# Piecewise first weight splits, woven indexer steps and merged short query tiles in a hybrid decoder step

## The chip, the cores and the metric

The kernel runs on one core of a Trainium2 chip. The metric is the device time of one execution, in microseconds (us). The core has five engines that run at the same time and meet at semaphores: TensorE (PE: matrix products and transposes; its weight loads are listed as PEld), VectorE (DVE), ScalarE (ACT), GpSimd (POOL) and SyncE (SP, which here only issues DMAs). DMA queues move data between HBM, the large memory, and SBUF, the working memory of 128 partitions; matrix products land in PSUM.

## The reference

One inference step of a two-layer decoder trunk. A prompt of 512 tokens and eight sample sequences of 8 new tokens each (576 tokens in all) go through the same weights; each sample also has 2048 past tokens in paged caches.

```python
D_MODEL, SEQ, DEPTH, DEC_BATCH, DEC_SEQ, PAST_LEN, HEAD_DIM, N_HEADS, H_IDX, D_FF = 1024, 512, 2, 8, 8, 2048, 64, 16, 8, 2816
# layer 0: one input projection -> mixer A (indexer-selected attention, 8 heads) beside mixer B (dilated windows, 8 heads)
# layer 1: one input projection -> mixer C (compressed, selected-block and window branches, 16 heads, gated)
# after each mixer: output projection, layer norm, ConvFFN, layer norm

def dsa_attend(q, qi, wi, q_pos, k, v, ki, tab):          # mixer A; its scores are the indexer
    s = jnp.einsum('bqhe,ble->bqhl', qib, ki) * (D_IDX ** -0.5)
    score = jnp.einsum('bqhl,bqh->bql', jax.nn.relu(s), wib) * (H_IDX ** -0.5)
    score = jnp.where(kpos <= pb, score, -jnp.inf)
    _, idx = lax.top_k(score, top)                        # then softmax attention over the picked keys

def masked_softmax(logits, mask):                         # all mixers; logits carry a bias by distance
    m = jnp.max(logits); p = jnp.exp(logits - m) * mask
    return p / jnp.sum(p)

def ab_project(x, w_in): ... split_cols(x @ w_in, AB_SPLITS)       # c_project likewise
# ConvFFN: up-projection to 2*2816, causal conv of width 3, gelu(gate) * value, down-projection
```

## The kernel before

**Phases.** The kernel is a chain of phases, one after another, with a barrier of all engines at the end of each: `proj_ab` (input projection of layer 0, with the set-up of the whole kernel in front), `tok_ab` (turns some results token-major), `idx` (the indexer), `sb` and `sa` (sample attention of B and A), `pab` (prompt attention of A and B), `out_ab`, `ffn0`, `proj_c`, `tok_c` and a compression step, `pc` (prompt attention of C), `sc` (sample attention of C), `out_c`, `ffn1`. Time saved inside one phase moves all later ones forward.

**Products in three parts.** A float32 product is made from three reduced ones (`split_product`, line 230): high weight by high input, high by low, low by high. The high part of a weight is a cast by ACT, the low part is what the cast left over, a subtraction by DVE (`low_part`, line 227, both of its inputs in SBUF). In `project_phase` ACT casts a group of 128x2048 weights in `split_high` (line 335), DVE subtracts in `split_low`, and `column_block` runs the 48 matmuls (8 k-tiles, 3 products, 2 halves) of 128 output columns, two such blocks to a group. `ffn_phase` has the same pair (line 2189) and `up_block`. PE waits for the whole group's low part before its first matmul. In `proj_ab` POOL meanwhile adds three rows of position tables in the set-up (line 222, 16x2952 each, also from two SBUF operands).

**Indexer (`indexer_phase`).** The past keys of eight samples are gathered page by page by POOL (line 493, eight gathers into four slots); the first four are issued in `tok_ab`. Sixteen half-samples are turned (`turn`, PE), copied (DVE), multiplied with the queries (`dot`, PE) and passed through ReLU (ACT). After every four halves `head_sums` adds the heads into a PSUM bank, DVE copies it to `part` (`copy_part`, line 1047, two buffers), and SP stores it to HBM and loads it back in another order (line 928, eight DMAs each time) into the score rows; there are four such parts in turn, and SP waits for each store to land before its loads. Between them SP issues the first key and value loads of `sb`. After the halves come 24 prompt steps (`prompt_dots`, `p_relu`, and a multiply-add on DVE, line 1071), and then SP stores the prompt scores (line 932). The phase ends when all of it is done.

**Prompt attention (`prompt_attention_phase`, for `pab` and `pc`).** Work units are (pair of heads, query tile i of 128 tokens, part); tile i sees (i+1)x128 keys. `pab` has 8 pairs with one part, `pc` 8 pairs with two. In round u PE runs `scores(u)`, `turn(u-2)` and `values(u-3)`; DVE runs `shift(u)` (line 742, adds the bias, takes the row maximum) and `weigh(u-1)` (a reciprocal at line 754, then scaling at line 759 or 762); ACT copies the turned weights (`copy_turned`, line 714) and runs the exponentials (line 725). `logit` and `shifted` are two deep, `tps` one. The order on each engine is the order of these loops:

```python
for u in range(U + 3):
    if u < U:
        scores(u)
    if 2 <= u < U + 2:
        turn(u - 2)
    if u >= 3:
        values(u - 3)
```

Of the kernel before, what the change touches and what calls it, by code (L numbers as in the profile page):

```python
# [21 lines left out]
P = 128  # L22
# [220 lines left out]

def project_phase(nc, name, w_in, cols, hT, keep, late_stores=(), late_loads=None, setup_of=None, ring=None):
# [8 lines left out]
    with phase(nc, name) as p:  # L253
# [12 lines left out]
        zero_set = p.sem("zero_set")  # L266
        setup = None if setup_of is None else Setup(nc, p, *setup_of)
# [32 lines left out]
        def column_block(pe, n, s, lo, slot):  # L300

            pe.wait_ge(copied0, n + 1)
            pe.wait_ge(copied1, n + 1)
            out = (acc[slot][0][:, 0:TH], acc[slot][1][:, 0:TH])
            for k in range(KC):
                last = split_product(pe, out, wh[:, s, k, lo:lo + P], wl[:, s, k, lo:lo + P], halves(keep.xh, k), halves(keep.xl, k),
                                     k == 0, k == KC - 1)
            last.then_inc(done, 1)

        @block.tensor  # L310
        def _(pe):
# [5 lines left out]
            with pe.Fori(0, loops) as i:  # L317
# [10 lines left out]
        def split_high(act, g, i, s, first=False):  # L328
# [6 lines left out]
            act.copy(wh[:, s, :, :], w[:, s, :, :]).then_inc(high, 1)  # L335

        def split_low(dve, g, s):
# [32 lines left out]
        def _(dve):  # L370
# [9 lines left out]
            for s in range(2):  # L380
                split_low(dve, s, s)
# [18 lines left out]
def token_major_phase(nc, name, hT, pieces, tok, keep, ahead=None):  # L400

    chunks = [(r0 + o, min(P, n - o), c0 + o) for r0, n, c0 in pieces for o in range(0, n, P)]
    with phase(nc, name) as p:
# [14 lines left out]
        if ahead is not None and ahead.other_queues:  # L418
# [36 lines left out]
class IndexerInputs:  # L455
# [3 lines left out]
    SLOTS = 4  # L459
# [129 lines left out]
def prompt_attention_phase(nc, name, pre, tok, keep, tok_loads=(), late=(), sel_bias=None, ahead=None, next_w=None):  # L589
# [3 lines left out]

    with phase(nc, name) as p:
# [3 lines left out]
        per_pair = NQ * parts  # L598
# [4 lines left out]
        nmax = p.sb("nmax", [P, 2, 2])  # L603
        total = p.sb("total", [P, 3, 2])
        weight = p.sb("weight", [P, 3, 2])
# [6 lines left out]
        units = [(m, i, part) for m in range(len(pairs)) for i in range(NQ) for part in range(parts)]  # L612
        U = len(units)
        block = p.body.enter_context(nc.Block())

# [32 lines left out]
        def _(pe):  # L648
            def scores(u):
                m, i, part = units[u]  # L650
                br, h = pairs[m][2][part]
                L = (i + 1) * P
                sel = branches[br]["sel"] and i > 0
                if u == 0:
                    pe.wait_ge(k_scaled, len(branches))
                if i == 0 and part == 0:
# [3 lines left out]
                for hd in range(2):  # L660
                    r = slice(hd * HD, (hd + 1) * HD)
                    mm = pe.matmul(logit[u % 2][hd][:, 0:L], q[m % 3][r, i * P:(i + 1) * P], kT[r, br, key_group(br, h), 0:L],
                                   start=True, stop=not sel)
                    if not sel:
                        mm.then_inc(logit_ready, 1)
                if sel:
                    for hd in range(2):
                        pe.matmul(logit[u % 2][hd][:, 0:L], keep.ident_bf[:, :], sel_bias[:, i - 1, 0:L],
                                  start=False, stop=True).then_inc(logit_ready, 1)

            def turn(u):
                i = units[u][1]
# [3 lines left out]
                for hd in range(2):  # L676
                    for kt in range(i + 1):
# [3 lines left out]
            def values(u):  # L681

                m, i, part = units[u]
# [5 lines left out]
                if m >= 2 and i == 0 and part == 0:  # L689
                    pe.wait_ge(mixed, m - 1)  # L690
                for kt in range(i + 1):
                    for hd in range(2):
                        g = (h + hd) // (b["heads"] // b["kv"])
                        v = tok[:, kt, b["v"] + g * HD:b["v"] + (g + 1) * HD]
                        last = pe.matmul(out[m % 2][hd * HD:(hd + 1) * HD, i * P:(i + 1) * P], v, pT[:, u % 2, hd, kt * P:(kt + 1) * P],
                                         start=(part == 0 and kt == 0), stop=(part == parts - 1 and kt == i))
# [11 lines left out]
        def _(act):  # L708
            def copy_turned(u):
                L = (units[u][1] + 1) * P  # L710
# [5 lines left out]
            for u in range(U + 2):  # L716
                if u >= 2:
                    copy_turned(u - 2)
                if u < U:
                    L = (units[u][1] + 1) * P  # L720
# [2666 lines left out]
```

## Time and profile before

| what | value |
|---|---|
| three runs | 2223.28, 2229.28, 2230.35 us, median 2229.28 |
| profiled execution | 2230.6 us, its span 2228.7 us, mean granted TensorE clock 0.938 |
| busy in the span | PE 1993.0 us (89%), DVE 1226.7 (55%), ACT 894.5 (40%), POOL 152.6 (7%) |
| stages, us from the start | proj_ab 0 to 183, idx 211.9 to 277.8, pab 494 to 577.7, ffn0 648 to 1114, proj_c 1115 to 1218, pc 1285 to 1436, ffn1 1767 to 2228 |

A row of the timeline gives the start, the duration, the engine with line and operation, output and inputs by name, shapes, how many instructions stand in the row, and in brackets how long the engine had been idle before and what ended that idle time. Matmuls overlap their successors a little, so the cost of one is read from start to next start. A busy engine is not always the bound; which wait ends last in a stage decides what a change there is worth.

### The profile page before, as it was taken

The numbers are of one execution on the slowest core, as the hardware profiler recorded it, in microseconds if no ns is written. First come the engines' busy times: TensorE is split into PE (matmuls) and PEld (weight loads), VectorE is DVE, ScalarE is ACT, GpSimd is POOL, SyncE is SP. The second block draws the span as 40 slices with busy tenths as digits, with TensorE's granted clock in tenths as the row PEclk, the third lists the DMA queues.
The fourth block names the chain that finished last, engine by engine and source line by source line (L and its number), as shares of the span: only waits on it lengthen the run. The fifth ranks groups of instructions, "written<-read, shape, count | busy, mean of one in ns | idle before, by whom it ended". The sixth has DMA issues, their size and how long they took to land. (4 is left out here: it accounts for less than half of the span.)

```text
span 2228.7 us, 40474 instructions
## 1 busy us (share of the span) xinstructions
PE 1993.0 (89%) x15280; PEld 1639.3 (74%) x15288; DVE 1226.7 (55%) x2551; ACT 894.5 (40%) x1520; POOL 152.6 (7%) x445
## 2 busy tenths in 40 slices
PE   7995688679879999999898699999998799999997
PEld 5994366445569999966598656667775699999765
DVE  4223598797565555544621478745444655555445
ACT  2120355347424445433221277644442244444332
POOL 4001200100001111100000000001100011111000
PEclk8997899879999999999899589999998899999998
DMA  5447699643226665532133563044313256664422
GB/s 155 140 155 254 180 379 356 229 142 120 76 65 206 219 203 201 178 106 79 57 125 89 164 209 88 27 161 163 137 53 114 65 189 202 217 208 162 125 79 71
DMA packets 170269, 342.80 MB, mean 154 GB/s; under 512 B 38494, under 2 KB 107150, under 8 KB 166138
## 3 DMA queue, kind: packets, MB, share of 16 engines
q1 hardware_dynamic: 155038, 201.85, 28.7%
q10 hardware_dynamic: 11132, 84.13, 11.1%
q0 software_dynamic: 3968, 55.06, 6.3%
q8 instruction: 85, 1.39, 0.3%
q14 instruction: 46, 0.38, 0.1%
HBM read 313.44 MB, written 98.40 MB: 185 GB/s over the span
## 5 line engine op out<-in xcount | busy, mean ns | idle before, releaser
L235 PE MATMUL ffn_acc<-x_h,ffn_wh 128*128 128x288 f32 x1408 | 303.5, 297 | 12.5 <-DVE ffn_wl L227 12.5
L235 PE MATMUL ffn_acc<-x_l,ffn_wh 128*128 128x288 f32 x1408 | 302.9, 297 | 0.0
L235 PE MATMUL ffn_acc<-x_h,ffn_wl 128*128 128x288 f32 x1408 | 302.8, 297 | 0.0
L235 PEld LDWEIGHTS ffn_acc<-x_h,ffn_wh 128*128 128x128 f32 x1408 | 228.2, 190 | 13.2 <-DVE ffn_wl L227 13.1
L235 PEld LDWEIGHTS ffn_acc<-x_l,ffn_wh 128*128 128x128 f32 x1408 | 228.3, 190 | 0.0
L235 PEld LDWEIGHTS ffn_acc<-x_h,ffn_wl 128*128 128x128 f32 x1408 | 228.2, 190 | 0.0
L227 DVE TENSOR_TENSOR ffn_wl<-ring,ffn_wh 128x2048 fp32r<-128x2048 f32 (+1 forms) x88 | 154.3, 1755 | 74.5 <-ACT ffn_wh L2189 74.5
L2135 PE MATMUL ffn_acc<-ffn_wh,x_h 128*128 128x512 f32 x352 | 144.6, 411 | 7.8 <-DVE ffn_wl L227 7.8
L2206 ACT COPY ffn_ext<-ffn_acc 128x288 f32<-128x288 f32 x88 | 35.4, 402 | 272.3 <-PE ffn_acc L235 269.9
L2137 PE MATMUL ffn_acc<-ffn_wh,x_l 128*128 128x512 f32 x352 | 140.6, 399 | 0.0
L2136 PE MATMUL ffn_acc<-ffn_wl,x_h 128*128 128x512 f32 x352 | 140.2, 398 | 0.0
L227 DVE TENSOR_TENSOR x_l<-ffn_hid,x_h 128x1024 fp32r<-128x1024 f32 x44 | 53.9, 1225 | 149.9 <-ACT x_h L2246 149.9
L2300 DVE COPY ffn_ext<-ffn_acc 128x224 f32<-128x224 f32 x88 | 34.1, 387 | 156.2 <-PE ffn_acc L235 156.2
L2246 ACT CAST x_h<-ffn_hid 128x1024 fp32r<-128x1024 f32 x44 | 46.2, 1049 | 163.6 <-PE ffn_acc L1761 161.6
L2135 PEld LDWEIGHTS ffn_acc<-ffn_wh,x_h 128*128 128x128 f32 x352 | 68.3, 194 | 34.9 <-issue 21.2
L235 PE MATMUL proj_ab_acc<-x_h,proj_ab_wh 128*128 128x288 f32 x368 | 80.1, 300 | 8.8 <-DVE proj_ab_wl L227 8.8
L2306 DVE SCALAR_TENSOR_TENSOR mixT<-ffn_ext,ffn_par_slot,mixT 128x592 f32<-128x592 f32 x88 | 73.2, 831 | 24.2 <-ACT mixT L2214 24.1
L2189 ACT CAST ffn_wh<-ring 128x2048 fp32r<-128x2048 f32 x44 | 83.8, 1910 | 2.6 <-PEq L2080 2.6
L2214 ACT ACTIVATE mixT<-ffn_ext,ffn_par_slot 128x592 f32<-128x592 f32 x88 | 72.6, 873 | 27.2 <-issue 27.2
L235 PE MATMUL proj_ab_acc<-x_h,proj_ab_wl 128*128 128x288 f32 x368 | 79.9, 299 | 0.0
L235 PE MATMUL proj_ab_acc<-x_l,proj_ab_wh 128*128 128x288 f32 x368 | 79.8, 299 | 0.0
L2137 PEld LDWEIGHTS ffn_acc<-ffn_wh,x_l 128*128 128x128 f32 x352 | 67.8, 193 | 15.2
(454 smaller groups left out, 4110.3 us busy)
## 6 DMA issues: line engine op xcount, KB each, us to landing
out_s_b_kv<-state_b_kv ACTq DMA_DIRECT2D x80, 768.0 KB, 8.0
ring<-ffn_up SPq DMA_DIRECT2D x44, 1024.0 KB, 5.3
ring<-ffn_down SPq DMA_DIRECT2D x44, 512.0 KB, 3.4
sb_k<-state_b_kv SPq DMA_DIRECT2D x8, 2048.0 KB, 10.7
sb_v<-state_b_kv SPq DMA_DIRECT2D x8, 2048.0 KB
proj_ab_w<-w_in_ab SPq DMA_DIRECT2D x11, 1024.0 KB, 5.4
ring<-w_in_c SPq DMA_DIRECT2D x7, 1024.0 KB, 5.4
hT_ab<-proj_ab_stage ACTq DMA_DIRECT2D x22, 288.0 KB, 2.1
```

Of the source, the lines that this page charges most:

```text
L227: return dve.tensor_tensor(low, whole, high.bitcast(F32), ALU.subtract)
L235: done = pe.matmul(o, weights, x, start=start, stop=stop)
L2135: pe.matmul(down_acc[t][:, :], part[0], wide[0], start=(f == 0), stop=False)
L2136: pe.matmul(down_acc[t][:, :], part[0], wide[1], start=False, stop=False)
L2137: last = pe.matmul(down_acc[t][:, :], part[1], wide[0], start=False, stop=(f == NF - 1))
L2189: act.copy(wh[:, s, :, :], w[:, s, :, :]).then_inc(w_high, 1)
L2206: act.copy(ext[:, e, 2:2 + TH], acc[e][:, 0:TH]).then_inc(main_out, 1)
L2214: act.activation(conv[:, e, :], ext[:, e, 0:CV], ACT.Identity, scale=par_slot[:, e, 0:1], bias=par_slot[:, e, 3:4]).then_inc(conv1, 1)
L2246: act.copy(hh[:, n % 3, :, 0:SEQ], hid[:, 2 * f2:2 * f2 + 2, 0:SEQ]).then_inc(d_high, 1)
L2300: dve.tensor_copy(ext[:, e, 2 + TH:S0], acc2[e][:, 0:SEQ - TH]).then_inc(small_out, 1)
L2306: dve.scalar_tensor_tensor(out=conv[:, e, :], in0=ext[:, e, 1:1 + CV], scalar=par_slot[:, e, 1:2], in1=conv[:, e, :], op0=ALU.mult, op1=AL ...
```

## The change

1. **Pieces.** In both projections and both feed-forward steps the first weight group is cast and subtracted in four pieces of two k-tiles each (128x512), each with its own semaphore step; PE's first block waits for the piece that it needs. In `project_phase` the first pass of PE's loop is written out ahead of the loop. All later groups stay whole.
2. **Woven indexer.** The 24 prompt steps run as 12 pairs between the sample halves, on PE, ACT and DVE, with buffers of their own. `part` and the bank of the head sums become single: `copy_part(u)` waits until part u-1 has been stored, and `head_sums(u)` until it has been copied. SP stores the prompt scores ahead of the last part instead of at the end, and half of the last part's loads go to ACT's queue. Only two of the first four gathers are issued in `tok_ab`, the other two at the start of `idx`.
3. **Merged short tiles.** In prompt attention query tiles 0 and 1 become one unit of three 128-key blocks: three units for each pair and part instead of four. The score matmuls, the shifts, the exponentials and the scalings stay one for each tile and head; the reciprocal, the copy of the turned weights and the semaphore rounds are made once for the merged unit.

```diff
+PIECES = 4
+def piece(n):
+    return slice(n * KC // PIECES, (n + 1) * KC // PIECES)
...
-        def column_block(pe, n, s, lo, slot):
+        def column_block(pe, n, s, lo, slot, in_pieces=False):
...
             for k in range(KC):
+                if in_pieces and k % 2 == 0:
+                    if k < KC - 2:
+                        pe.wait_ge(first_low, k // 2 + 1)
+                    else:
+                        pe.wait_ge(low, 3)
...
-            with pe.Fori(0, loops) as i:
+            for s in range(2):
+                if s:
+                    pe.wait_ge(low, s + 3)
+                for j in range(2):
+                    column_block(pe, 2 * s + j, s, j * P, 2 * s + j, in_pieces=(s == 0 and j == 0))
+            with pe.Fori(1, loops) as i:
...
-            act.copy(wh[:, s, :, :], w[:, s, :, :]).then_inc(high, 1)
-        def split_low(dve, g, s):
+            if first and s == 0:
+                for n in range(PIECES):
+                    k = piece(n)
+                    act.copy(wh[:, s, k, :], w[:, s, k, :]).then_inc(first_high if n < PIECES - 1 else high, 1)
+            else:
+                act.copy(wh[:, s, :, :], w[:, s, :, :]).then_inc(high, 1)
+        def split_low(dve, g, s, first=False):
+            if first and s == 0:
+                for n in range(PIECES - 1):
+                    k = piece(n)
+                    dve.wait_ge(first_high, n + 1)
+                    low_part(dve, wl[:, s, k, :], w[:, s, k, :], wh[:, s, k, :]).then_inc(first_low, 1)
...
-                ahead.gather(pool, range(ahead.SLOTS))
+                ahead.gather(pool, range(ahead.FIRST))
...
-    SLOTS = 4
+    SLOTS, FIRST = 4, 2
...
+    TILES_OF = ((0, 1), (2,), (3,))
+    AT = (0, P, 0, 0)
...
-        units = [(m, i, part) for m in range(len(pairs)) for i in range(NQ) for part in range(parts)]
+        units = [(m, tiles, part) for m in range(len(pairs)) for tiles in TILES_OF for part in range(parts)]
...
             def turn(u):
-                i = units[u][1]
                 pe.wait_ge(scaled, 2 * (u + 1))
...
-                    for kt in range(i + 1):
+                    for kt in range(blocks(u)):
                         last = pe.transpose(tps[:, hd, kt * P:(kt + 1) * P], probs[:, u % 3, hd, kt * P:(kt + 1) * P], keep.ident[:, :])
...
-                dve.reciprocal(weight[:, u % 3, :], total[:, u % 3, :]).then_inc(weighed, 1)
+                dve.reciprocal(weight[:, u % 3, 0:N, :], total[:, u % 3, 0:N, :]).then_inc(weighed, 1)
...
-        part = p.sb("part", [P, 2, 512])
+        part = p.sb("part", [P, 512])
...
-        p_relu = relu[:, :, :].rearrange("p s (f c) -> p (s f) c", f=2)
+        p_relu = p.sb("p_relu", [P, 3, 512])
...
                 if u == 3:
                     ahead.load_values(sp)
+                    for i in range(1, NQ):
+                        L = (i + 1) * P
+                        sp.wait_ge(p_summed, len(steps) + i)
+                        sp.dma_start(pscore[:, i - 1, 0:L], p_score[:, i - 1, 0:L]).then_inc(p_stored, 16)
                 sp.wait_ge(part_done, u + 1)
...
+                load_rows(sp, u, 0)
+                if u + 1 < NB // 2:
+                    load_rows(sp, u, 1)
...
             for n in range(N + 1):
+                if n == 0:
+                    pe.wait_ge(inputs.prompt_in, 48)
+                    prompt_dots(0)
                 if n < N:
                     turn(n)
                 if n >= 1:
                     dot(n - 1)
                 if n >= 5 and n % 4 == 1:
                     head_sums(n // 4 - 1)
+                if 1 <= n < PAIRS:
+                    prompt_dots(n)
...
+            act.wait_ge(parts_stored, 16 * (NB // 2))
+            load_rows(act, NB // 2 - 1, 1)
...
             def copy_part(u):
                 dve.wait_ge(sum_done, u + 1)
-                if u >= 2:
-                    dve.wait_ge(parts_stored, 16 * (u - 1))
+                if u:
+                    dve.wait_ge(parts_stored, 16 * u)
...
             for n in range(1, N):
                 copy_turned(n)
                 if n >= 6 and n % 4 == 2:
                     copy_part(n // 4 - 1)
+                if n <= PAIRS:
+                    add_heads(n - 1)
...
-            up_block(0, 0, 0)
+            up_block(0, 0, 0, in_pieces=True)
```

In `ffn_phase`, `split_high`, `split_low` and `up_block` are edited as in `project_phase`.

## Rows read from the trace of the kernel before

**Rows 1.** Windows, pc stage: busy us (instructions) per engine, PEclk, DMA share, GB/s

```profile
1285.00:1436.30 151.30, 142.54 (x1216) 88.53 (x1216) 118.50 (x456) 114.54 (x320) 2.00 (x2) 0.97 0.38 110
```

**Rows 2.** Timeline and page: starts of ffn1, of both ffn steps together, of proj_c

```profile
1767.40 3.70 ACT L2189 CAST ffn_wh<-ring 128x2048 fp32r<-128x2048 f32 x2 [1.25 <-PEq L2080]
...
1769.34 4.49 DVE L227 TENSOR_TENSOR ffn_wl<-ring,ffn_wh 128x2048 fp32r<-128x2048 f32 x2 [2.46 <-ACT ffn_wh L2189]
...
1771.68 0.85 PE L235 MATMUL ffn_acc<-x_h,ffn_wh 128*128 128x288 f32 x2 [6.16 <-DVE ffn_wl L227]
...
L235 PE MATMUL ffn_acc<-x_h,ffn_wh 128*128 128x288 f32 x1408 | 303.5, 297 | 12.5 <-DVE ffn_wl L227 12.5
...
1119.48 0.82 PE L235 MATMUL proj_c_acc<-x_h,proj_c_wh 128*128 128x288 f32 x2 [6.46 <-DVE proj_c_wl L227]
```

**Rows 3.** Timeline, set-up of proj_ab: one 128x512 cast and one 128x512 low part

```profile
17.75 0.59 ACT L193 CAST x_h<-proj_ab_acc 128x512 fp32r<-128x512 f32 x1 [10.86 <-PE proj_ab_acc L171]
...
18.37 0.69 DVE L227 TENSOR_TENSOR x_l<-proj_ab_acc,x_h 128x512 fp32r<-128x512 f32 x1 [1.11 <-ACT x_h L193]
```

**Rows 4.** Line 222 on POOL, and timeline of DVE and PE, start of proj_ab

```profile
L222 POOL TENSOR_TENSOR proj_ab_vec<-proj_ab_vec,proj_ab_base x3: 6407/6456/8535, 17.3 to 30.2; 16x2952 f32<-16x2952 f32 x3
...
27.16 13.68 DVE L227 TENSOR_TENSOR proj_ab_wl<-proj_ab_w,proj_ab_wh 128x2048 fp32r<-128x2048 f32 x2 [2.07 <-ACT proj_ab_wh L335]
...
32.59 0.82 PE L235 MATMUL proj_ab_acc<-x_h,proj_ab_wh 128*128 128x288 f32 x2 [8.83 <-DVE proj_ab_wl L227]
33.20 0.68 PE L235 MATMUL proj_ab_acc<-x_l,proj_ab_wh 128*128 128x288 f32 x2
33.68 0.68 PE L235 MATMUL proj_ab_acc<-x_h,proj_ab_wl 128*128 128x288 f32 x2
...
39.39 0.43 PE L235 MATMUL proj_ab_acc<-x_h,proj_ab_wh 128*128 128x288 f32 x2
39.66 0.42 PE L235 MATMUL proj_ab_acc<-x_l,proj_ab_wh 128*128 128x288 f32 x2
```

**Rows 5.** Line 493 on POOL in tok_ab: issues, landing; PE's first instruction in idx

```profile
L493 POOL DMA_INDIRECT idx_kidx<-cache_a_kidx,chunk_row x4: 933/941/1142, 201.3 to 205.3; - x4
...
DMA to landing us min/median/max: 6.2/6.2/6.4
...
211.97 1.94 PE L946 MATMUL idx_tps<-ident,idx_kidx 128*128 128x128 f32 x8 [10.10 <-PEq L104]
```

**Rows 6.** idx: waits (us, times, longest) of DVE; timeline of SP's last DMAs

```profile
DVE idx_part L1047 <- DMA idx_parts<-idx_part: 6.1, 1, 6.1
...
271.65 2.67 SPq L928 DMA_DIRECT2D select_work<-idx_parts  x8
274.36 1.30 SPq L932 DMA_DIRECT2D pscore<-idx_p_score  x3
```

**Rows 7.** Timeline of PE, steps of one pab pair

```profile
511.64 0.87 PE L678 MATMUL pab_tps<-ident,pab_probs 128*128 128x128 f32 x6 [0.88 <-DVE pab_probs L759]
512.45 0.66 PE L695 MATMUL pab_out<-pab_pT,v_tok 128*64 128x128 f32 x8
...
516.34 0.44 PE L678 MATMUL pab_tps<-ident,pab_probs 128*128 128x128 f32 x2
516.71 1.09 PE L695 MATMUL pab_out<-pab_pT,v_tok 128*64 128x128 f32 x16
...
518.80 0.66 PE L678 MATMUL pab_tps<-ident,pab_probs 128*128 128x128 f32 x4
519.38 0.44 PE L695 MATMUL pab_out<-pab_pT,v_tok 128*64 128x128 f32 x4
519.75 0.49 PE L662 MATMUL pab_logit<-spare 64*128 64x128 f32 x4
```

**Rows 8.** Waits of PE in the two prompt stages (us, times, longest)

```profile
PE pab_tps L678 <- DVE pab_probs L759: 7.2, 8, 1.2
...
PE pc_tps L678 <- DVE pc_probs L762: 6.2, 16, 0.9
```

More of the change, by code:

```diff
@@ L681, in values @@
             def values(u):
-                m, i, part = units[u]
+                m, tiles, part = units[u]
                 br, h = pairs[m][2][part]
@@ L688, in values @@
                 pe.wait_ge(copied, u + 1)
-                if m >= 2 and i == 0 and part == 0:
+                if m >= 2 and tiles[0] == 0 and part == 0:
                     pe.wait_ge(mixed, m - 1)
[L691 to L696, printed above, removed]
+                for i in tiles:
+                    for kt in range(i + 1):
+                        for hd in range(2):
+                            g = (h + hd) // (b["heads"] // b["kv"])
+                            v = tok[:, kt, b["v"] + g * HD:b["v"] + (g + 1) * HD]
+                            at = AT[i] + kt * P
+                            last = pe.matmul(out[m % 2][hd * HD:(hd + 1) * HD, i * P:(i + 1) * P], v, pT[:, u % 2, hd, at:at + P],
+                                             start=(part == 0 and i == 0), stop=(part == parts - 1 and kt == NQ - 1))
                 last.then_inc(out_ready, 1)
@@ L730, in shift @@
             def shift(u):
-                m, i, part = units[u]
-                L = (i + 1) * P
-                if i == 0 and part == 0:
+                m, tiles, part = units[u]
+                if tiles[0] == 0 and part == 0:
                     dve.wait_ge(t_in[m % 3], 16 * (m // 3 + 1))
@@ L1007, in _ @@
+                if n == PAIRS + 2:
+                    pe.wait_ge(new_relu, 1)
+                    pe.wait_ge(built, 4)
+                    for b in range(NB):
+                        last = pe.matmul(sums_new, w_new[:, b, :], relu_new[:, b, :], start=(b == 0), stop=(b == NB - 1), tile_position=(0, TS))
+                    last.then_inc(new_sums, 1)
+            head_sums(NB // 2 - 1)
         @block.scalar
         def _(act):
-            for n, (b, f) in enumerate(halves):
-                act.wait_ge(dot_done, n + 1)
-                if n >= 4:
-                    act.wait_ge(sum_done, n // 4)
-                act.activation(relu[:, b % 2, f * 512:(f + 1) * 512], dots[n % 2][:, :], ACT.Relu, scale=IDX_SCALE).then_inc(relu_done, 1)
@@ L1084, in _ @@
+            copy_part(NB // 2 - 1)
             dve.wait_ge(rows_in, 16 * 4 * NB)
@@ L2188, in split_high, with split_low @@
             act.wait_ge(up_done, g * 2 + 2)
-            act.copy(wh[:, s, :, :], w[:, s, :, :]).then_inc(w_high, 1)
-        def split_low(dve, g, s):
+            if first and s == 0:
+                for n in range(PIECES):
+                    k = piece(n)
+                    act.copy(wh[:, s, k, :], w[:, s, k, :]).then_inc(first_high if n < PIECES - 1 else w_high, 1)
+            else:
+                act.copy(wh[:, s, :, :], w[:, s, :, :]).then_inc(w_high, 1)
+        def split_low(dve, g, s, first=False):
+            if first and s == 0:
+                for n in range(PIECES - 1):
+                    k = piece(n)
+                    dve.wait_ge(first_high, n + 1)
+                    low_part(dve, wl[:, s, k, :], w[:, s, k, :], wh[:, s, k, :]).then_inc(first_low, 1)
+                k = piece(PIECES - 1)
+                dve.wait_ge(w_high, 1)
+                low_part(dve, wl[:, s, k, :], w[:, s, k, :], wh[:, s, k, :]).then_inc(w_low, 1)
+                return
             dve.wait_ge(w_high, g + 1)
```

259 lines of the change are left out of this document (137 added, 122 removed).

## Prediction, made before the changed kernel was run

> **What bounds the kernel now.** I read the stages first. They follow each other behind barriers, so whatever a stage loses from its own path is lost from the whole. Then I read, in each edited stage, which wait ends last. In the pc stage PE is busy 142.5 of 151.3 us, while DVE and ACT are at 118.5 and 114.5 [rows 1]: PE sets the pace there, and the question is what PE waits for. At the start of a projection or feed-forward step PE waits for the low part of its first weights and for nothing else [rows 2]. In idx no engine is the bound: DVE stands 6.1 us for a store of parts to land, and the stage ends with SP's serial loads and stores [rows 6]. In the two prompt stages PE's main wait is for the scaled weights that it is to turn [rows 8]. So four places are to be worked out; the first three are small, the fourth carries most of the sum.
>
> **Pieces in ffn0, ffn1 and proj_c.** In ffn1 the cast starts at 1767.40, the low part at 1769.34 and PE at 1771.68, which is 4.28 us from the first cast to the first matmul [rows 2]. A piece is 128x512: 0.59 us on ACT, 0.69 us on DVE, with 18.37 - 17.75 = 0.62 us from the start of the cast to that of the subtraction [rows 3]. With 0.05 us for the step to PE the new start comes after 0.62 + 0.69 + 0.05 = 1.36 us, so 2.92 us are gained. Later pieces cost nothing that is seen: DVE finishes one each 0.69 us, while PE works 12 matmuls on one, at a pitch of 0.24 us early in a stage (33.20 to 33.68 is two) and 0.134 later (39.39 to 39.66 is two) [rows 4], hence 2.9 or 1.6 us. The four casts take 4 x 0.59 = 2.4 us in place of 1.9, the subtractions 2.8 in place of 2.3; that pushes the second group by half a us, and the cover is the two blocks of the first group, 96 matmuls or more than 12 us. The other two starts have the same shapes and waits: both ffn steps together idle 12.5 us at this wait, proj_c 6.46 us [rows 2]. Sum for three starts **-8.8 us** (from -7.5 to -9).
>
> **Pieces in proj_ab.** This start looks like the others and isn't. DVE took 13.68 us for two low parts [rows 4] that take 4.49 in ffn1 [rows 2], and PE started at 32.59. Meanwhile POOL ran its three table additions, from 17.3 on, of 6.41, 6.46 and 8.54 us, the last one from 30.2 to 38.7 [rows 4]. The long one is 2.1 us longer than the others, about one low part; the first low part ended just ahead of 32.59, that is 2.3 us after the second addition; the second low part ended at 40.84, about 2.2 us after the third. So the two engines take turns by whole instructions: a waiting low part gets its turn when an addition ends, and when it ends the waiting addition goes ahead of the next low part. With pieces the same order gives: piece 0 waits until 30.2 and ends at 30.9, PE starts at 30.95 instead of 32.59, the third addition runs from 30.9 to 37.3, and piece 1 ends at 38.0. PE has done its 12 matmuls by 33.8 and stands until 38.05. Before the change it had done (38.05 - 32.59) / 0.24 = 22.7 by then, so it is now 10.7 behind, 1.4 us at the fast pitch. The pause of 4.2 us can also set the clock back: PE idles ahead of every slow start in these rows. Before, the slow pitch lasted at most from 32.59 to 39.39; a second slow stretch of up to 6 us costs 0.44 us per us, so up to 2.6 us more. I take the middle of 1.4 and 4.0: **+2.7 us**, a loss. The other end is a sharing of the path in proportion to time: then piece 0, released 1.94 - 0.62 = 1.3 us earlier, takes a quarter of the first low part's 5.4 us, and the change gains 1.3 + 4.1 = 5.4 us; between these, if DVE kept its turn for all four pieces, PE would start at 30.95 and gain 1.6.
>
> The Trainium skill says of this, on the page "SBUF — State Buffer", section "Who interferes with whom", that a VectorE instruction with two SBUF inputs and a GpSimd instruction that reads SBUF exclude each other for a whole instruction, and that the one issued first goes first. The 2.1 us above agree with that; it speaks against cutting a blocked instruction into four, since each cut is a place where the other may go first, and by it the start is lost, where by sharing it is won by 5.4 us.
>
> **Two gathers fewer ahead of idx.** POOL's four gathers go out from 201.3 to 205.3, 1.25 us or more apart, and each lands 6.2 us after its issue, the last at 211.5; PE's first instruction in idx is at 211.97, after 10.1 us of idling at the barrier [rows 5]. Everybody else is done by then. With two gathers the last one lands near 209.0, so idx starts **2.5 us** earlier (0 if the barrier hangs on something not seen, 3 at best). The two moved gathers are issued on POOL at the start of idx and are wanted only from the fifth half-sample on.
>
> **Woven indexer.** It takes the prompt steps into the gaps of the sample halves. But the stage's end hangs on SP: store a part, wait for the landing, load it back, four times, with the first loads of sb in between, and DVE's wait of 6.1 us for such a landing [rows 6] shows that compute is ahead of the chain even unwoven. Woven halves are slower, so the first part comes about 1 us later (0 to 2.5). With one `part` buffer the third copy on DVE waits for the second store; the fourth copy is queued behind it, and the prompt additions are done by then, so nobody else loses. The prompt scores' three DMAs, 1.30 us of issue [rows 6], move ahead of the last part's store, about 1.5 us with their transfer; the end loses them, and half of the last eight loads (2.67 us [rows 6]) goes to ACT's queue, 1.3 us less. Copy and landing at the end stay. I take 1 + 1.5 - 1.3 - 0.8, the last for the landing of the prompt scores that no longer ends the stage: **+0.4 us** (-2 to +3).
>
> **Merged short tiles.** A matmul step costs from start to next start: the turn of tile 0 0.37, of tile 1 0.58, of six blocks 0.81 [rows 7]; so the merged turn saves 0.14. For the values step (tile 0: 0.37 [rows 7]) I take the same 0.14, and for the scores, which stay separate matmuls, 0.05 (0 to 0.2). That is 0.33 us of PE per merged unit. The larger part is the wait. In pab PE stands about 0.9 us in each pair ahead of the turn of tile 2 (511.64 [rows 7]; eight waits, 7.2 us [rows 8]): these weights are scaled only after DVE has shifted tile 3, and between the end of tile 3's scores (518.80) and that turn PE has just the turn of tile 1, the values of tile 0 and the scores of tile 0, 0.58 + 0.37 + 0.5 = 1.45 us [rows 7]. With the wait that makes 2.3 us, which DVE needs. With the merged unit PE has a turn of 0.81, the values of tile 3 (about 1.0, as at 516.71 [rows 7]) and the scores of two tiles (0.9 to 1.1) in that time, near 2.8 us, so the wait goes. pab: 8 x (0.33 + 0.9) = 9.8, less 1 us since the first, larger unit fills the pipeline later: -8.8. In pc there are two merged units to a pair, 0.66 us, and PE is idle 8.8 us in all [rows 1], 1.1 per pair, 6.2 of them in this wait [rows 8]; the two units of tile 3 still follow each other on DVE, so I let 0.6 of the 1.1 go: 8 x 1.26 - 1 = -9.1. Together **-17.9 us**; by PE's steps alone it is 8 x 0.99 - 2 = -6; if all idle time in pc went, -22.
>
> **Sum.** -8.8 + 2.7 - 2.5 + 0.4 - 17.9 = -26.1. The profiled execution took 2230.6 us, 1.3 more than the median of 2229.3, and its span covers all but 2 us of it; from it 2204.5, from the median **2203 us**.
>
> **Rivals.** (a) The merged units save PE's steps and no waits: DVE's shift of two tiles, two heads each, comes in one lump, and PE waits for that instead. For it: in pc DVE is at 78% [rows 1]; against it: the wait is tied to one place in the pair, which the order changes. -6 in place of -17.9: 2215. (b) The ports are shared, or DVE keeps its turn, in proj_ab: 4.3 to 8.1 us better, 2195 to 2199. For it only that the blocking has one instance here. (c) The weave shortens idx after all, because parts come earlier in step with the loads of sb: I let it take twice the wait of 6.1 us [rows 6], 12: 2191. Against it: that wait itself, which says that compute is early. (d) Slower: merged rounds become bound by the chain of one unit. With `logit` and `shifted` two deep, two rounds must hold scores, shift, exponential, scaling, turn, copy and values. PE's three steps are about 2.6 us; DVE's and ACT's share is 118.5 and 114.5 us over 48 rounds [rows 1], 2.5 and 2.4. Half of 7.5 is 3.75 us a round: pc 48 x 3.75 = 180 (+29), pab 24 x 3.75 = 90 (+6), and the 17.9 is lost: 2256. It decides once a round takes over some 3.4 us on the mean of 72 rounds (now 235 us, 3.26 each); against it, the same two buffers serve today's units of tile 3, the widest, and PE is still busy for 94% of pc. (e) The barrier ahead of idx doesn't move: 2206, inside the range.
>
> **How the numbers follow.** Chances: forecast with (e) 0.60, (a) 0.14, (b) 0.15, (c) 0.07, (d) 0.04. The range goes from 2190 to 2216: it takes in (a), (b) and (c), and the bounds of idx and proj_ab about the forecast. A measurement of this kernel can tell about 0.3%, 6.7 us, from no change: same is 2222.6 to 2236. Only (d), or (a) with every small term at its bad end, gets there: faster 0.94, same 0.03, slower 0.03.
>
> **What would show it.** PE's idle time ahead of its first matmul falls from about 6.3 to 3.4 us in ffn0, ffn1 and proj_c. In proj_ab PE starts near 31 and then stands some 4 us after 12 matmuls, while line 222 shows one addition between the first and the second piece; if PE runs through, the taking of turns is refuted. PE's first instruction in idx comes 10 us, less 2.5, after the last of tok_ab. idx keeps its 66 us within 3; if it falls below 60, (c) is right. The wait for scaled weights goes from 7.2 us to under 1 in pab, and to about 2 in pc; the stage lengths fall by 9 each. The prediction is wrong above all if that wait stays or returns in another place.

## The result and the profile after

The changed kernel takes 2196.6 us in the median (four runs, 2186.7 to 2199.2) against 2229.4 us before; the ratio is 0.985, 95% interval 0.982 to 0.987. The forecast was 2203 us with a range from 2190 to 2216. The profiled execution took 2195.1 us with a span of 2193.2, 35.5 less than before.

The stages, from barrier to barrier, say where this came from. All kernels of the study stand in one table, one profiled execution of each, since the later sections read from it. The pitch is the time from one matmul's start to the next one's in the steady part of a stage. In the two projections and the two feed-forward steps a star marks a pitch of 0.130 us; without a star it was 0.133 (the last section is about this).

| kernel | proj_ab | tok_ab | idx | pab | ffn0 | proj_c | pc | ffn1 |
|---|---|---|---|---|---|---|---|---|
| before | 186.0 | 25.9 | 65.9 | 83.6 | 466.7 | 106.2 | 151.6 | 461.6 |
| after | 184.3* | 23.0 | 71.5 | 73.7 | 461.8 | 103.6 | 137.1 | 457.6 |
| e1 merged tiles only | 185.0 | 25.6 | 65.8 | 73.4 | 459.5* | 106.2 | 139.2 | 459.5 |
| e2 pieces only | 188.8 | 26.2 | 64.8 | 83.6 | 463.7 | 100.8* | 150.9 | 449.9* |
| e3 indexer only | 184.9 | 23.1 | 71.1 | 83.5 | 466.5 | 104.0* | 152.3 | 454.8* |
| e4 after, proj_ab whole | 184.7 | 23.5 | 71.4 | 73.7 | 454.9* | 103.6 | 137.9 | 451.8* |
| e5 after, additions held | 178.3 | 23.1 | 71.4 | 73.7 | 461.8 | 103.6 | 138.0 | 457.0 |
| e6 after, loads early | 188.3 | 23.3 | 64.9 | 73.7 | 462.6 | 103.1 | 137.0 | 456.9 |
| e7 after, old indexer | 188.3 | 23.3 | 65.9 | 73.7 | 461.8 | 103.6 | 138.1 | 449.9* |
| e8 additions held, loads early | 179.4 | 23.2 | 62.9 | 73.7 | 454.7* | 103.6 | 138.0 | 457.8 |
| e9 e8, values last | 177.5 | 23.3 | 55.7 | 73.7 | 461.8 | 101.2* | 138.0 | 456.8 |
| e10 after, scores last | 188.2 | 23.2 | 69.8 | 73.7 | 454.9* | 103.7 | 138.0 | 456.8 |
| e11 after, again | 188.6 | 23.3 | 71.7 | 73.7 | 461.9 | 103.6 | 138.0 | 449.9* |

From before to after: pc -14.5, pab -9.9, ffn0 -4.9, ffn1 -4.0, tok_ab -2.9, proj_c -2.6, proj_ab -1.7, and idx +5.6. The stages not listed add -0.6.

**The starts.** This is the changed kernel's timeline of ACT and DVE in ffn0 and of PE in proj_c and ffn1, with the page's row for both feed-forward steps (start, duration, instruction, count, and in brackets the idle time before and what ended it). They answer to [rows 2].

```profile
640.17 2.18 ACT L2265 CAST ffn_wh<-ring 128x512 fp32r<-128x512 f32 x4 [1.32 <-PEq L2148]
...
640.83 2.50 DVE L227 TENSOR_TENSOR ffn_wl<-ring,ffn_wh 128x512 fp32r<-128x512 f32 x4 [1.18 <-ACT ffn_wh L2265]
...
L235 PE MATMUL ffn_acc<-x_h,ffn_wh 128*128 128x288 f32 x1408 | 303.0, 297 | 6.8 <-DVE ffn_wl L227 6.8
...
1103.59 0.82 PE L235 MATMUL proj_c_acc<-x_h,proj_c_wh 128*128 128x288 f32 x2 [3.48 <-DVE proj_c_wl L227]
...
1737.52 0.82 PE L235 MATMUL ffn_acc<-x_h,ffn_wh 128*128 128x288 f32 x2 [3.36 <-DVE ffn_wl L227]
```

PE's wait went from 12.5 to 6.8 us in the two feed-forward steps together and from 6.46 to 3.48 in proj_c: 2.8 to 3.0 us for each start. The four subtractions follow each other without a gap and stay ahead of PE.

**proj_ab.** Line 222 on POOL (count, shortest, median and longest duration in ns, first and last start) and the timeline of PE, changed kernel, beside [rows 4].

```profile
L222 POOL TENSOR_TENSOR proj_ab_vec<-proj_ab_vec,proj_ab_base x3: 6407/6451/6882, 17.0 to 29.8; 16x2952 f32<-16x2952 f32 x3
...
30.57 0.82 PE L235 MATMUL proj_ab_acc<-x_h,proj_ab_wh 128*128 128x288 f32 x2 [7.55 <-DVE proj_ab_wl L227]
...
33.11 0.68 PE L235 MATMUL proj_ab_acc<-x_h,proj_ab_wl 128*128 128x288 f32 x2
37.33 0.85 PE L235 MATMUL proj_ab_acc<-x_h,proj_ab_wh 128*128 128x288 f32 x2 [3.54 <-DVE proj_ab_wl L227]
...
41.00 0.42 PE L235 MATMUL proj_ab_acc<-x_h,proj_ab_wl 128*128 128x288 f32 x2
```

PE starts at 30.57, does 12 matmuls, stands until 37.33 and is fast only near 40.5, where it was fast by 39.4 before. The longest addition is now 6.88 us instead of 8.54: it was held up by one piece and not by a whole low part, and piece 1 came when it had ended, at 29.8 + 6.9 = 36.7.

**idx.** Timeline of PE and SP, and the waits of DVE and SP (total, times, longest), changed kernel, beside [rows 5] and [rows 6]. The three rows at the end are of the kernel before: PE's first product with the queries, its first head sums, and SP's first store.

```profile
207.38 1.22 PE L1039 MATMUL idx_p_dots<-idx_ki,idx_qi 64*128 64x256 f32 x4 [7.40 <-PEq L104]
...
213.15 2.05 PE L1018 MATMUL idx_dots<-idx_kT,idx_q_blk 128*128 128x512 f32 x2 [2.65 <-DVE idx_w_sel L1113]
...
225.04 1.05 PE L1028 MATMUL idx_sums<-idx_relu,idx_w_sel 128*16 128x512 f32 x8
...
228.88 0.36 SPq L990 DMA_DIRECT2D idx_parts<-idx_part  x1
230.92 5.53 SPq L964 DMA_DIRECT2D select_work<-idx_parts  x8
...
243.52 4.59 SPq L990 DMA_DIRECT2D idx_parts<-idx_part  x1
254.54 2.98 SPq L964 DMA_DIRECT2D select_work<-idx_parts  x8
...
263.43 1.76 SPq L988 DMA_DIRECT2D pscore<-idx_p_score  x3
265.23 0.45 SPq L990 DMA_DIRECT2D idx_parts<-idx_part  x1
274.49 1.31 SPq L964 DMA_DIRECT2D select_work<-idx_parts  x4
...
DVE select_score L1152 <- DMA select_work<-idx_parts: 16.1, 1, 16.1
...
SPq L964 <- DMA idx_parts<-idx_part: 18.6, 4, 8.8
...
217.72 2.05 PE L956 MATMUL idx_dots<-idx_kT,idx_q_blk 128*128 128x512 f32 x2 [3.81 <-DVE idx_w_sel L1051]
...
226.57 1.05 PE L966 MATMUL idx_sums<-idx_relu,idx_w_sel 128*16 128x512 f32 x8
...
229.56 0.36 SPq L921 DMA_DIRECT2D idx_parts<-idx_part  x1
```

PE enters idx after 7.4 us of idling in place of 10.1. DVE's wait of 16.1 us for the last loads is followed only by the copy that ends the stage, so all other compute is over when it begins. Nothing was gained by that, since the second store is issued at 243.5 and its loads begin at 254.5, and the fourth store at 265.2 with its loads at 274.5. SP's chain is the stage. The prompt steps did not go into idle time everywhere: from PE's first product to its first head sums it is 11.9 us in place of 8.9, since PE has no gap there, and four pairs of prompt products stand in between.

**Prompt attention.** Windows of pab and pc (us, busy us and instructions of PE, PEld, DVE, ACT, POOL, then PEclk, DMA share, GB/s), PE's waits, and PE's timeline through the two merged units of one pc pair, changed kernel, beside [rows 1, 7, 8].

```profile
496.00:569.70 73.70, 70.22 (x632) 46.34 (x632) 56.44 (x224) 55.89 (x152) 0.00 (x0) 0.96 0.34 114
1269.00:1406.00 137.00, 130.82 (x1216) 87.39 (x1216) 115.15 (x440) 110.58 (x304) 2.00 (x2) 0.99 0.43 121
...
PE pc_tps L721 <- DVE pc_probs L813: 4.4, 9, 1.7
...
PE pab_tps L721 <- DVE pab_probs L810: 1.6, 4, 0.5
...
1333.20 0.93 PE L704 MATMUL pc_logit<-pc_kT,pc_q 64*128 64x128 f32 x8
1334.31 1.09 PE L721 MATMUL pc_tps<-ident,pc_probs 128*128 128x128 f32 x8 [0.18 <-DVE pc_probs L813]
1335.33 0.88 PE L740 MATMUL pc_out<-pc_pT,tok_c 128*64 128x128 f32 x12
1336.13 0.93 PE L704 MATMUL pc_logit<-pc_kT,pc_q 64*128 64x128 f32 x8
1336.99 1.09 PE L721 MATMUL pc_tps<-ident,pc_probs 128*128 128x128 f32 x8
```

In pc PE is now busy for 130.8 of 137.0 us. Its wait for scaled weights fell from 6.2 to 4.4 us, and most of what is left stands at the ends of the stage: from 1290 to 1390 it is 1.0 us in six waits (before, 4.2 us in twelve, from 1306 to 1420). In pab the same wait fell from 7.2 to 1.6 us. The merged scores take 0.86 us from start to next start (1336.13 to 1336.99), the merged turn and values 0.8 each in other rounds.

### The profile page after: what moved, and what is told of

It is laid out like the page before. It is cut to its first block and busy times, and to the rows that moved or that the text cites. A ratio compares the mean times of both kernels' runs of the same rounds, so it can differ in the third digit from the quotient of the medians.

```text
span 2193.2 us, 40283 instructions
## 1 busy us (share of the span) xinstructions
PE 1966.9 (90%) x15288; PEld 1623.0 (74%) x15288; DVE 1222.0 (56%) x2538; ACT 888.9 (41%) x1508; POOL 150.8 (7%) x445
## 5 line engine op out<-in xcount | busy, mean ns | idle before, releaser
L227 DVE TENSOR_TENSOR ffn_wl<-ring,ffn_wh 128x1024 fp32r<-128x1024 f32 (+2 forms) x94 | 154.9, 1653 | 73.6 <-ACT ffn_wh L2267 71.2
```

Of the source, the lines that this page charges most:

```text
L227: return dve.tensor_tensor(low, whole, high.bitcast(F32), ALU.subtract)
```

## The experiments

**Theories.** A: each part acts by itself; the merged tiles take out PE's steps and waits; the pieces gain at three starts and lose in proj_ab, where POOL and DVE take turns; the indexer is SP's chain, and weaving is a loss with this order of loads. The rivals to it stand with each run.

**e1, the merged tiles alone** on the kernel before (third point of the change, nothing else).

> The kernel before with the merged short tiles alone. Theory A, the waits of PE go and each part of the change acts by itself: pab falls from 83.6 to 73.7 us and pc from 151.4 to 136.9 as in the changed kernel, 24 us in all, about 2205 us. Rival B, part of the 24 us comes from the earlier start or from the other edits (the shape of the stages before): pab and pc together fall by 18 us or less, about 2212 us.

Measured: 2200.8 us, ratio 0.987 (0.981 to 0.992). pab takes 73.4 us and pc 139.2, together 22.6 less than before, where the changed kernel has 24.4 less. Theory A holds to 2 us, and these two stages are about two thirds of the 35.5 us between the two profiles.

**e2, the pieces alone** on the kernel before (first point, nothing else).

> The kernel before with the first weight groups in pieces alone (both projections, both feed-forward steps). Theory A: the first matmul of ffn0, ffn1 and proj_c comes 2.9 us earlier and the three stages are 3 to 3.5 us shorter each; in proj_ab PE starts near 30.6, works 12 matmuls and stands 3.5 us until POOL's third addition is over. Whether proj_ab's steady pitch is 0.130 us as in the changed kernel or 0.133 as in the one before is open: if the pitch belongs to the code, proj_ab ends about 1 us earlier than before, about 2218 us in all; if it changes from execution to execution, proj_ab ends some 2 us later, about 2221. Rival B, the early start is used up inside the stage by the loads: less than 2 us for each start, above 2223.

Measured: 2224.0 us, ratio 0.999 (0.997 to 1.001); nothing that the whole time can tell; by its number it would be rival B, above 2223. The stages speak for A. Line 222 and PE's second piece in this run:

```profile
L222 POOL TENSOR_TENSOR proj_ab_vec<-proj_ab_vec,proj_ab_base x3: 6412/6439/6882, 17.0 to 29.8; 16x2952 f32<-16x2952 f32 x3
...
37.31 0.85 PE L235 MATMUL proj_ab_acc<-x_h,proj_ab_wh 128*128 128x288 f32 x2 [3.54 <-DVE proj_ab_wl L227]
```

The pause is the same as in the changed kernel, and with the pitch at 0.133 us proj_ab takes 188.8 us, 2.8 more than before. ffn0, at the pitch of before, is 3.0 us shorter, where rival B allowed less than 2. The other two starts can't be read from their stages here, as both ran at 0.130.

**e3, the indexer's edits alone** on the kernel before (second point, nothing else).

> The kernel before with the indexer's edits alone (woven steps, single part buffer, moved stores, two gathers ahead). Theory A, SP's chain of stores and loads sets the stage: idx starts 2.5 to 3 us earlier and takes 71 to 72 us in place of 66, so sb starts 2 to 3 us later, about 2232 us. Rival B, the weave pays and its gain was covered in the changed kernel by the shifted start: idx takes 66 us or less, about 2226 us.

Measured: 2232.0 us, ratio 1.001 (0.999 to 1.003). idx starts 2.8 us sooner after tok_ab began and takes 71.1 us. Theory A: the indexer's edits cost 5 us of the stage, in the kernel before as in the one after. The whole times of e1, e2 and e3 sum to some 25 us less, against 33 for the whole change, but e1's interval alone is 26 us wide; that the parts add up is read from the stages.

**e4, the changed kernel with proj_ab's first group whole** (`whole` is true in proj_ab alone; the last line stands for two alike, one for the cast and one for the subtraction).

```diff
+        whole = setup_of is not None
...
-                if s:
+                if s or whole:
                     pe.wait_ge(low, s + 3)
                 for j in range(2):
-                    column_block(pe, 2 * s + j, s, j * P, 2 * s + j, in_pieces=(s == 0 and j == 0))
+                    column_block(pe, 2 * s + j, s, j * P, 2 * s + j, in_pieces=(not whole and s == 0 and j == 0))
...
-            if first and s == 0:
+            if first and s == 0 and not whole:
```

> The changed kernel, but in proj_ab the first weight group stays whole (the loop's first pass stays written out). Theory A, taking turns with POOL makes the pieces there a loss: PE starts near 32 and doesn't stand after 12 matmuls, proj_ab ends 1 to 3 us earlier, about 2194 us. Rival B, the pieces gain there by the earlier start: proj_ab ends 1 to 4 us later, about 2199 us. If the pitch is 0.130 us here too, it comes with the written-out pass or from elsewhere, not from the pieces.

Measured: 2194.6 us, ratio 0.986 (0.983 to 0.990). proj_ab takes 184.7 us at a pitch of 0.133. All five runs with pieces and that pitch (e2, e6, e7, e10, e11) have 188.2 to 188.8, all four with a whole group (before, e1, e3, e4) 184.7 to 186.0. So the pieces cost some 3 us there. That the changed kernel's own profile shows 184.3 is the pitch of 0.130: e11 has the same code and 188.6. The longest addition is 8.56 us again.

```profile
L222 POOL TENSOR_TENSOR proj_ab_vec<-proj_ab_vec,proj_ab_base x3: 6412/6457/8562, 17.6 to 30.4; 16x2952 f32<-16x2952 f32 x3
```

**e5, the additions held back.** The cause itself is moved: POOL's second and third addition wait until DVE has done its first two groups.

```diff
-    def gpsimd(self, pool, zero_set):
+    def gpsimd(self, pool, zero_set, low):
...
         for k in range(3):
+            if k == 1:
+                pool.wait_ge(low, 4)
             pool.tensor_tensor(self.vec[:, k, :], self.vec[:, k, :], self.base[:, :], ALU.add).then_inc(self.vec_done, 1)
```

> The changed kernel, but POOL's second and third table additions in proj_ab wait until the low parts of the first two weight groups are done. Theory A, POOL and DVE take turns by whole instructions and nothing else delays the pieces: the first addition ends near 23.5, the four pieces follow each other on DVE without a gap, PE starts near 26.5 and doesn't stand after 12 matmuls, so the first block's copy on DVE comes near 37 us in place of 43.9 (a steady pitch of 0.130 or 0.133 us over the stage moves its end by 3 us more, whatever the kernel). Rival B, DVE's subtraction is slow there for another reason (the loads of the next weights, say): PE starts at 30 or later as before.

Measured: 2188.7 us, ratio 0.982 (0.978 to 0.986). Timeline of DVE, PE and POOL, in this order (L229 and L224 are the lines 227 and 222 of the other kernels):

```profile
25.31 2.50 DVE L229 TENSOR_TENSOR proj_ab_wl<-proj_ab_w,proj_ab_wh 128x512 fp32r<-128x512 f32 x4 [0.79 <-ACT proj_ab_wh L360]
28.68 2.29 DVE L229 TENSOR_TENSOR proj_ab_wl<-proj_ab_w,proj_ab_wh 128x2048 fp32r<-128x2048 f32 x1 [0.87 <-ACT proj_ab_wh L362]
34.44 0.46 DVE L414 COPY proj_ab_stage<-proj_ab_acc 128x288 f32<-128x288 f32 x1 [3.47 <-PE proj_ab_acc L237]
...
26.15 0.50 PE L237 MATMUL proj_ab_acc<-x_h,proj_ab_wh 128*128 128x288 f32 x2 [2.98 <-DVE proj_ab_wl L229]
...
31.05 13.05 POOL L224 TENSOR_TENSOR proj_ab_vec<-proj_ab_vec,proj_ab_base 16x2952 f32<-16x2952 f32 x2 [7.33 <-DVE proj_ab_wl L229]
```

Without POOL the whole group takes DVE 2.29 us in place of 5.4 and 8.3, PE starts at 26.15, and proj_ab ends at 178.3 us, 10 earlier than with pieces and the additions where they were. The first block's copy comes at 34.4, even before the 37 that I had expected. Theory A stands: the subtraction is slow only beside POOL, and then by whole instructions.

**e6, sb's first loads earlier** in the woven indexer.

```diff
-                if u == 1:
+                if u == 0:
                     ahead.load_keys(sp)
+                if u == 2:
+                    ahead.load_values(sp)
                 if u == 3:
-                    ahead.load_values(sp)
                     for i in range(1, NQ):
```

> The changed kernel, but SP issues the first key loads of sb ahead of the first part's store and the first value loads ahead of the third's, in place of the second and fourth. Theory A, the woven indexer's gain is hidden by SP's chain, in which the second and fourth stores stand behind 2.5 MB of loads: idx falls from 71.5 to 57 to 61 us, and about 2184 us in all if sb keeps its 126 us. Rival B, the transfers themselves fill the time and their order doesn't matter: idx stays at 69 us or more. Rival C, what idx gains sb gives back by waiting for its first values: idx and sb together fall by less than 5 us.

Measured: 2194.6 us, ratio 0.987 (0.983 to 0.991). idx takes 64.9 us: 6.6 less, but not the 10 to 14 of theory A, and sb is about as long as in the changed kernel (126.8 against 126.3). A's point that the order of loads matters holds, its size doesn't. e8, which has the same order, shows why.

**e7, the changed kernel with the indexer of before** (the two gathers still moved).

> The changed kernel with the indexer of before (the prompt steps after the sample halves, two part buffers, prompt scores stored last), two gathers still moved into idx. Theory A, the woven indexer is a loss with this order of loads: idx takes 65 to 67 us in place of 71.5 and still starts 2.5 us or more earlier than in the kernel before, about 2191 us. Rival B, the five us were chance or due to the gathers: idx takes 70 us or more here too.

Measured: 2196.2 us, ratio 0.988 (0.984 to 0.991). idx takes 65.9 us, and starts 23.3 us after tok_ab as in the changed kernel. So the gathers' gain of 2.6 to 2.9 us is their own, and the loss of 5.6 is that of the other indexer edits together: the weave, the single part buffer and the moved stores. The whole time, 2196.2 us and not the 2191 expected, doesn't show it; the stages do.

**e8, both edits** of e5 and e6.

> The two edits together: table additions held back in proj_ab, sb's first loads issued earlier in the woven indexer. Theory A: the gains of both add up, about 6 us in proj_ab and 10 to 14 us in idx, about 2179 us, faster than both kernels. Rival B: less than half of that is left.

Measured: 2183.2 us, ratio 0.981 (0.978 to 0.985), about 13 us under the changed kernel. proj_ab gains 8 to 9 us (179.4), idx 8.6 (62.9), less than the 10 expected. SP's timeline in idx:

```profile
223.78 0.35 SPq L993 DMA_DIRECT2D idx_parts<-idx_part  x1
232.34 3.90 SPq L966 DMA_DIRECT2D select_work<-idx_parts  x8
236.29 0.35 SPq L993 DMA_DIRECT2D idx_parts<-idx_part  x1
241.66 2.65 SPq L966 DMA_DIRECT2D select_work<-idx_parts  x8
244.36 0.60 SPq L1463 DMA_DIRECT2D sb_v<-state_b_kv  x1
...
246.88 0.61 SPq L993 DMA_DIRECT2D idx_parts<-idx_part  x1
254.81 2.67 SPq L966 DMA_DIRECT2D select_work<-idx_parts  x8
```

Two stores still wait 8 us to land: the first behind the keys, the third behind the values, which went on the queue 2.5 us ahead of it. Between the two, from 237.6 to 242.6, the DMA engines are busy to a share of 0.15.

**e9, the values last.** As e8, but the values go on the queue behind the last loads of parts.

```diff
-                if u == 2:
-                    ahead.load_values(sp)
...
                 if u + 1 < NB // 2:
                     load_rows(sp, u, 1)
+            ahead.load_values(sp)
```

> The kernel of the run e8_both, but SP issues sb's first value loads only behind the last loads of parts (the key loads stay ahead of the first store). Theory A, a part's store waits for whatever was put on SP's queue ahead of it: the third store no longer stands behind 2.5 MB of values, it lands 2 to 3 us after its issue in place of 8, and idx falls from 62.9 to 53 to 56 us; sb may give back up to 4 us by waiting for its first values, about 2177 us in all. Rival B, the transfers fill the time whatever their order: idx stays above 60 us. Rival C: sb gives back all that idx gains, about 2183 us.

Measured: 2173.0 us, ratio 0.979 (0.975 to 0.983): the fastest of the study, 24 us under the changed kernel.

```profile
243.54 0.34 SPq L991 DMA_DIRECT2D idx_parts<-idx_part  x1
245.62 2.66 SPq L966 DMA_DIRECT2D select_work<-idx_parts  x8
248.32 1.31 SPq L989 DMA_DIRECT2D pscore<-idx_p_score  x3
249.68 0.44 SPq L991 DMA_DIRECT2D idx_parts<-idx_part  x1
252.06 1.30 SPq L966 DMA_DIRECT2D select_work<-idx_parts  x4
```

The third store lands 2.1 us after its issue in place of 7.9, idx falls to 55.7 us, and sb takes 127.7 us against 128.6 in e8: it gives nothing back. Theory A for this store. Not every late landing is this queue's: the second store still takes 6.2 us to land in e9, though none of sb's loads went out between it and the first one. And that the woven steps pay now is not shown: no run has the indexer of before with this order of loads, so the gain of the order and a gain of the weave can't be told apart.

**e10, the prompt scores last** in the changed kernel.

> The changed kernel, but the prompt scores are stored last, as in the kernel before. Theory A, three DMAs ahead of the last part's store cost the chain about what they take to issue (1.8 us) and cost less at the end: idx 70 to 71 us in place of 71.5. Rival B, they cost more, since their 0.6 MB stand ahead of the store on the queue: idx 68 us or less. Rival C: stored last, their landing ends the stage, and idx takes 72 us or more.

Measured in a single run: 2195.1 us, idx 69.8 us. So the three stores cost the stage 1.7 to 1.9 us net by standing ahead of the last part; just under theory A's 70 to 71, and closest to it.

**e11, the changed kernel again.**

> The changed kernel once more, without an edit. Theory A, the steady pitch of the matmuls (0.130 or 0.133 us) is drawn anew in each stage of each execution: proj_ab shows 0.133 this time, or one of ffn0, proj_c and ffn1 shows 0.130; with 0.133 proj_ab ends near 187.5 us in place of 184.3. Rival B, the pitch belongs to the code: proj_ab 0.130 and the other three 0.133 again.

Measured in a single run: 2199.3 us. Windows in the steady part of proj_ab and of ffn1 (columns as above), first of the changed kernel's first profile, then of this one:

```profile
60.00:170.00 110.00, 110.00 (x849) 110.00 (x848) 28.86 (x27) 24.37 (x27) 0.00 (x0) 1.00 0.46 156
1800.00:2000.00 200.00, 200.00 (x1502) 200.00 (x1501) 112.13 (x173) 93.56 (x107) 25.82 (x128) 1.00 0.62 206
...
60.00:170.00 110.00, 110.00 (x827) 110.00 (x826) 26.81 (x26) 24.04 (x26) 0.00 (x0) 1.00 0.45 146
1800.00:2000.00 200.00, 200.00 (x1541) 200.00 (x1540) 115.81 (x176) 98.16 (x112) 26.40 (x128) 1.00 0.65 215
```

The same code, the same granted clock of 1.00 (2.4 GHz) and the same full PE, but proj_ab went from 849 matmuls in 110 us to 827, and ffn1 from 1502 in 200 us to 1541. Theory A: the pitch changes from execution to execution, stage by stage.

## Why the prediction was right, and where it was not

The time fell inside the range, 6.4 us under the forecast; from profile to profile it was 35.5 us against the 26.1 of the sum. Term by term:

- **Pieces at three starts, -8.8.** The wait fell as worked out, by 2.8 to 3.0 us each. The stages, at equal pitch, are shorter by 4.9 (ffn0), 4.0 (ffn1) and 2.6 us (proj_c): -11.5. Part of the 2.7 more is the clock: PE's slow stretch after the first matmul was 4.0 and 4.5 us in the two feed-forward steps before and 3.2 and 3.0 after (3.5 to 4.5 in all profiles with whole groups, 2.9 to 3.9 in all with pieces but e8's ffn1, 6.1), and a us less of it is worth 0.44. That leaves 1.7 us in ffn0 and 0.5 in ffn1 open, and scatter of one profile is as large: e2, with pieces alone, gained just 3.0 in ffn0, and ffn1, with a whole group and the same pitch, took 461.6 us before and 459.5 in e1.
- **proj_ab, +2.7.** Right in sign, place and size: +3 us by nine runs, with the start, the twelve matmuls, the pause and the second piece within 0.8 us of the forecast times. The view that decided was line 222's three durations in [rows 4]. Rival (b) is out, by e4 and e5. The changed kernel's first profile alone would have said -1.7 and hidden it.
- **Gathers, -2.5.** Measured -2.6 to -2.9.
- **Woven indexer, +0.4 with -2 to +3.** Measured +5.6, outside the bounds. The mechanism was right (SP's chain sets the end, compute waits), the sizes were off. The step "the first part comes about 1 us later (0 to 2.5)" failed: its store went from 17.7 us after the stage's start to 21.6, +3.9. PE was busy all the time there before as well (5.00 of 5.00 us from 221.9 on), so the prompt products were work put on the path: four pairs stand between PE's first product and its first head sums, 1.15, 0.64, 0.63 and 0.85 us, and DVE's copy of the part then comes 0.9 us later after the sums. The first pair ran at a granted clock of 0.50 (1.2 GHz, until 217), as the first rounds did before, so the clock explains only 0.5 us. The moved prompt scores cost the chain 2.4 us up to the last loads in place of 1.5, the stores between took 1.1 more that had no term, and the end gave back 1.8 where 1.3 + 0.8 was forecast: 3.9 + 2.4 + 1.1 - 1.8 = 5.6. Rival (c) is refuted in this kernel; in e9, with sb's loads out of the way, idx falls to 55.7 us, but how much of that is the weave's isn't shown.
- **Merged tiles, -17.9 with -6 to -22.** Measured -24.4, by e1 alone -22.6: the largest term, and too small. In pc a pair took 18.2 us before and 16.3 after, -1.85 where I had 1.26. The mis-sized step is PE's own: the busy time of such a pair fell by 1.2 us (17.33 to 16.12) where I had 0.66, the idle time by 0.65 (0.83 to 0.18) where I had 0.6. The scores of the merged unit take 0.86 us in place of 0.46 + 0.63, from start to next start in the timeline of before; I had let 0.05 of these go, and it was 0.23, so a merged unit saves about 0.5 us and not 0.33. In the whole of pc PE's busy time fell from 142.5 [rows 1] to 130.8 us and its idle time from 8.8 to 6.2, so the larger part was steps and not waits; some of it is the clock, granted at 0.50 for the first 10 us of the stage before and for the first 4 here. In e7, again with 10 us at 0.50, pc takes 138.1 us with PE busy for 133.0. The sign that the wait would fall to about 2 us in pc and under 1 in pab did not come: it is 4.4 and 1.6. In pab a pair fell by 1.45 us (9.48 to 8.03, early in the stage) against 1.23, of which 0.88 was the wait, as forecast. The 1 us per stage for the larger first unit was not separately seen.
- **Rivals.** (d) is refuted by e1, and so is (a): the two stages lost 22.6 us and not 6, and pab's wait went. In pc (a) was right that the steps count most, at about twice their price. (e) is refuted by all runs with two gathers.

The errors of the indexer (+5.2), of the merged tiles (-6.5) and of the starts (-2.7) partly cancel, to -4.0. Of the other 5.4 us, 4.4 are proj_ab, which had the pitch of 0.130 in this one profile, and the rest the gathers and the stages not listed. So the time was right by more than its steps deserve, and part of it is luck: three of the five terms ended outside their bounds.

## What to carry to other kernels

Look at which instruction each engine is on while a short one waits: cutting a blocked instruction into pieces gives the other engine more places to go first, and holding the other engine's work back by one semaphore gave 10 us where the pieces alone had cost 3. When a stage ends on a chain of small stores and loads, first ask what stands ahead of the store: here moving compute brought nothing while large loads stood there, and changing the order of the loads brought 16 us. And compare stages at equal pitch: with differences of 7 to 8 us in a single stage from one execution to the next, whole times can't tell parts of 3 to 5 us.

## What the runs showed of the hardware

**Two steady paces of TensorE at one granted clock.** The matmuls of 288 columns that follow each other in the projections and feed-forward steps came at 0.130 us in some stages and at 0.1333 in others, 2.6% apart, both at a granted clock of 1.00. Over 13 profiles proj_ab drew the faster one once, ffn0 four times, proj_c three times and ffn1 five times; e11 shows that the code doesn't decide it. In a feed-forward stage it is worth some 7 us. That it explains the 10 to 20 us by which runs of one kernel differ is not shown, since one execution of each kernel is profiled: from the changed kernel's first profile to e11 the paces alone would make it 3 us faster, and it was 4 us slower. At the slower pace three steps of 0.13 us are followed by one of 0.14. What sets it was not found.

**Taking turns.** At the start of proj_ab a VectorE subtraction with both inputs in SBUF and a GpSimd addition with both inputs in SBUF did not run side by side: the addition took 6.41 to 6.55 us alone, 8.54 to 8.56 with a whole low part ahead of it, 6.88 with a piece, and with both engines waiting it was the other one's turn each time. The subtraction of [rows 3], with one input in PSUM, took its 0.69 us beside the first addition [rows 4]. The Trainium skill, page "SBUF — State Buffer", section "Who interferes with whom", states the exclusion for a whole instruction; the trace agrees, with these numbers.
